# Starting the stationary weight units 128 bytes into their ring places instead of 64

## What is computed

```
h = rms_norm(x);  proj = h @ w_in            # 1024 x 8008: all inputs of three mixers and three gates
y_a = gated recurrence (hq, hf, hi, hg)      # 4 heads of 128
y_b = causal softmax attention (mq, mk, mv)  # 4 heads of 128
y_c = top-64 latent attention (dq, c_kv, indexer iq, ik, iw)
merged = sum over branches of sigmoid(gates) * (y @ w_branch)
x = x + rms_norm(merged @ w_out)
gate, up = split(rms_norm(x) @ w_ffn_in)     # 1024 x 5632
x = x + rms_norm((silu(gate) * up) @ w_ffn_out)   # 2816 x 1024
```

## Time and profile before

| | us |
|---|---|
| median of 3 runs | 463.78 |
| lowest, highest | 463.74, 463.91 |
| the profiled execution | 463.29 |
| its span, first to last instruction | 461.6 |
| TensorE busy | 454.1 |
| VectorE busy | 301.5 |
| ScalarE busy | 248.9 |
| DMA queue of the weights, share of 16 engines | 57.4% |

### The profile page before, as it was taken

The page is one execution under the profiler, slowest core; times in us unless marked ns, Lnnn a source line. Parts: engine busy times, 40 slices in busy tenths (PEclk is TensorE's granted clock), DMA queues, the critical chain, the costliest instruction groups (busy, mean ns, idle before and its releaser), DMA issues.

```text
span 461.6 us, 8038 instructions
## 1 busy us (share of the span) xinstructions
PE 454.1 (98%) x3318; PEld 400.3 (87%) x3318; DVE 301.5 (65%) x403; ACT 248.9 (54%) x370; POOL 49.1 (11%) x50
## 2 busy tenths in 40 slices
PE   8999999999999999999999999999999999999994
PEld 7799798987788888888888888999999999888883
DVE  4657689898628746577449797866565665743532
ACT  5768369338485955526443462855544554433410
POOL 2301002456630100000000000100000000000000
PEclk9999999999999999999999999999999999999999
DMA  8997665545434464569565544666666656766202
GB/s 296 398 296 221 187 172 179 173 130 159 148 125 135 140 183 136 184 186 322 190 210 186 184 168 148 216 192 189 188 191 207 192 187 188 247 200 186 89 0 91
DMA packets 26024, 85.60 MB, mean 185 GB/s; under 512 B 3171, under 2 KB 4740, under 8 KB 25988
## 3 DMA queue, kind: packets, MB, share of 16 engines
q1 hardware_dynamic: 25268, 84.31, 57.4%
q10 hardware_dynamic: 720, 0.79, 0.5%
HBM read 83.84 MB, written 1.25 MB: 184 GB/s over the span
## 4 chain that ended last, share of the span: by engine, by line
PE 97%; DVE 1%; DMA 1%; SPq 0%; ACT 0%; issue 0%; DVEq 0%
PE bank L1450 56%; PE bank L1444 31%; PE bank L1476 1%; PE bank L1620 1%; PE bank L1485 1%; DMA raw<-w_stream 1%; PE bank L1632 1%; PE bank L1660 1%; PE bank L1604 1%; PE bank L1584 1%; PE bank L1575 1%; PE bank L1521 1%; PE bank L1523 0%; PE bank L1526 0%; PE bank L1633 0%; PE bank L1664 0%
## 5 line engine op out<-in xcount | busy, mean ns | idle before, releaser
L843 DVE TENSOR_TENSOR wl<-raw,wh 128x1024 fp32r<-128x1024 f32 (+1 forms) x150 | 185.0, 1267 | 44.3 <-ACT wh L514 44.0
L514 ACT ACTIVATE wh<-raw 128x1024 fp32r<-128x1024 f32 (+1 forms) x150 | 153.5, 1049 | 83.7 <-PE bank L1450 42.0
L1444 PE MATMUL bank<-hTh,wh 128*128 128x256 f32 x416 | 116.2, 279 | 0.0
L1444 PE MATMUL bank<-hTl,wh 128*128 128x256 f32 x416 | 115.1, 277 | 0.0
L1444 PE MATMUL bank<-hTh,wl 128*128 128x256 f32 x416 | 115.1, 277 | 0.0
L1450 PE MATMUL bank<-wh,hTh 128*128 128x512 f32 (+1 forms) x216 | 85.4, 395 | 0.2 <-DVE wl L843 0.2
L1450 PE MATMUL bank<-wh,hTl 128*128 128x512 f32 (+1 forms) x216 | 83.0, 384 | 0.0
L1450 PE MATMUL bank<-wl,hTh 128*128 128x512 f32 (+1 forms) x216 | 83.0, 384 | 0.0
L1444 PEld LDWEIGHTS bank<-hTh,wh 128*128 128x128 f32 x416 | 78.1, 188 | 0.5 <-issue 0.3
L1444 PEld LDWEIGHTS bank<-hTh,wl 128*128 128x128 f32 x416 | 78.2, 188 | 0.1
L1444 PEld LDWEIGHTS bank<-hTl,wh 128*128 128x128 f32 x416 | 78.2, 188 | 0.0
(11 more groups left out here) (227 smaller groups left out, 528.7 us busy)
## 6 DMA issues: line engine op xcount, KB each, us to landing
raw<-w_stream SPq DMA_DIRECT2D x146, 512.0 KB, 4.1
raw<-w_stream SPq DMA_DIRECT2D x4, 328.0 KB, 6.5
x<-x_in SPq DMA_DIRECT2D x4, 256.0 KB, 4.2
raw<-w_stream SPq DMA_DIRECT2D x4, 256.0 KB, 4.3
bias<-bias_scratch SPq DMA_DIRECT2D x8, 128.0 KB, 4.8
x<-x_in SPq DMA_DIRECT2D x1, 1024.0 KB, 5.7
out<-mo SPq DMA_DIRECT2D x3, 256.0 KB, 2.0
post<-post_mix ACTq DMA_DIRECT2D x1, 512.0 KB, 9.8
```

What stands on the lines that cost most here:

```text
L514: did(act.activation(wh[:, u % SPLIT, place(u)], raw[:, u % RING, place(u)], ACT.Copy), high_done, u + 1 - EARLY)
L843: did(dve.tensor_tensor(wl[:, u % RING, place(u)], raw[:, u % RING, place(u)], wh[:, u % SPLIT, place(u)].bitcast(F32), ALU.subtract), low ...
L1444: ins = pe.matmul(bank[bk][:, i * S:(i + 1) * S], w_[:, k, h * P:(h + 1) * P], x_[:, kt, :], start=first, stop=final, skip_group_check=True)
```

## The change

SHIFT becomes 32 elements, so the 53 shifted units begin 128 bytes into their places, at a multiple of 256 bytes. The two unused tensors took their size from SHIFT and now have it written out, so they stay 64 bytes, and no other tensor moves. Count, order, shape and waits of all instructions are the same on each engine.

```diff
-SHIFT, PLACE = 16, 1024 + 64
+SHIFT, PLACE = 32, 1024 + 64
...
-        skip = [sb("skip0", [P, SHIFT])]
+        skip = [sb("skip0", [P, 16])]
...
-        skip.append(sb("skip1", [P, SHIFT], stack=early))
+        skip.append(sb("skip1", [P, 16], stack=early))
```

## The result

| | before | after |
|---|---|---|
| median of 4 runs, us | 463.76 | 470.35 |
| lowest, highest | 463.68, 463.91 | 469.22, 471.16 |
| profiled execution, its span | 463.29, 461.6 | 471.11, 469.4 |

The change makes the kernel slower: the ratio is 1.0139, 95% interval 1.0123 to 1.0154. The forecast was 463.8 us with a range to 467.8, so the time lies outside it.

What follows compares the result with a forecast made beforehand. TensorE was taken to bound the kernel, by matmul count times pace. All terms of the change were 0, so the profiled execution stayed at 463.29 us and the median, 0.49 above, at 463.8 us; range 463.0 to 467.8.

Steps and rivals of the forecast that it cites:

- What bounds the kernel: Whole kernel: TensorE, busy 454.1 of 461.6 us; time is the number of matmuls by their pace.
- ACT, DVE, DMA at 0: ACT's copy, DVE's subtraction and the DMAs of moved units: the new address costs TensorE 0.
- rival E: DMAs: 16 transactions instead of 17 per 4096 bytes, landings below 4.1 us, time still 463.8; within the 0.68 for no change.
- Weight loads at 0: Weight loads at lines 1444 and 1575: the new start address and changed distance between read streams cost 0.
- The room for a load: Matmul loop: a load slower by more than some 3.4 ns would set the pace, now 113.4 ns.
- Rival B: Lines 1444 and 1575: the address slows every load; 5.0 us more, 468.8 or above; chance 0.11, including a load still slower.
- Rival A: Line 1444's long stretch of 864 matmuls falls to 117.9 ns each: 3.9 us more, 467.7; chance 0.14.
- Rival D: Moved matmuls: the pace itself falls by 6.7 ns each, 8.5 us less, 455.3; chance 0.05, including other gains over 0.93 us.

Runs made afterwards that it cites:

- split matmuls: Each line 1444 matmul split into two of 128 columns with own weight loads, in the kernel before and the changed one: 601.78 and 600.66 us.

## Why the prediction was wrong

**What bounds the kernel**: right. The whole effect is in the pace of TensorE at lines 1444 and 1575, and every other piece of the chain kept its length.

**ACT, DVE, DMA at 0**: right. 1057 and 1219 ns, no new wait of TensorE for either. Landings late in the kernel take 3.5 to 3.6 us in place of 4.1 to 4.3, the sign that I gave for rival E, but the units that were not moved show the same, and the kernel before with one transpose more has 4.1 in one stretch of moved units and 3.5 in another, so it is not the start address. TensorE waited for none of them.

**Weight loads at 0**: this is the step that failed, in two of its parts. "I take 0, since the two start addresses that the rows do show cost the same to the nanosecond" rested on the 188 ns of the earlier trace rows. That number stays 188 ns when the loop slows from 113.4 to 118.7 ns, so it could not have shown a price. And the second part, "I see no conflict between the streams", compared line 1444 at a distance of 64 with line 1450 at 0 and found the same time for a column. That these two are equal says only that each form was at a distance that suits it: the runs show 120.0 ns for line 1444 at 0, and 52.70 us in place of 51.90 for line 1450 at 64. An equality between two forms was read as independence within each.

**The room for a load**: 3.4 ns in my text, from a row of transposes. The split matmuls give 1.7 ns, if the load sets their pace.

**Rival B** is what came, with another cause. It priced the 1104 quick matmuls at 4.5 ns each, 468.8 or more; they lost about 5.2 ns each, and the 168 slow ones nearly 2 ns, 6.0 us in all. Its mark, a load longer than 188 ns, is not there. I gave it 0.11 because the load looked equal at two addresses.

**Rival A**, that the long piece can fall into the other pace and that this is worth 3.9 us, is real: 3.8 us, in the pair with hTh moved. What turns it is open. It is not what the change did. At 128 bytes there is no quick pace to fall out of.

**Rival D** fell. The quick pace never went under 113.3 ns.

The rule of the Trainium skill (TensorE: Matmul & The Clock Gate, Step-by-step: what each phase is for) that loading the next weights doesn't steal bandwidth from the running matmul, by which any address has price 0, agrees with the loads of the split run and not with the full stream, where only the distance of the two operands was changed and the matmul's step went from 113.4 to 120.0 ns. The measurement decides: in this loop the pace depends on where the two operands lie relative to each other.

## What to carry to other kernels

Where a weight load takes nearly as long as the columns that move beside it, the start addresses of the two operands relative to each other can be a tuning knob, worth 4 to 6% of TensorE's pace in this loop; try several distances and look for steps at the columns' own pace. Read it from start to start over a long piece, not from the duration of single loads or matmuls. Keep the distance the same when tensors are rearranged: a harmless move of an unrelated tensor can change it. And if equal loops of one kernel show two paces, a small edit elsewhere may go with a change of pace in them: read every piece of the chain before putting a difference down to the edit.

## What was unexpected in the hardware

The pace of 256-column matmuls with a 128 x 128 load each, in fp32r, depends on the distance of the operands' starts in steps as fine as 16 bytes: 113.3 ns at 64 bytes, 118.8 at 80, 120.0 at 0. It repeats with 256 bytes at least in this sense: units lie in places that are 256 bytes apart modulo 512, and within one run the step is 120 ns in all of them. At 64 bytes the loop has two steady paces, and it kept the one it had after its first few steps for 98 us or more, over 864 matmuls and across 36 units. What in the memory or in TensorE makes 64 the good distance for one form of product and 0 for the other stays open; the runs show the dependence, not its cause. Also open is whether some distance between those tried has the quick pace in every piece. In the kernel before that would be worth 0.76 us more, too little to tell from no change.
